# Two changes at once: expert weights loaded in 2 MB units of 16 KB per partition, and the recurrence's gate matmuls spread between the first block's projections

## What is computed

```python
def first_block(x, ...):
    h = rmsnorm(x, norm1_g)
    p = einsum('bsd,dn->bsn', h, w_in)                  # 1024 -> 1536
    lru_x, lru_gate, four_in = p[..., :512], p[..., 512:1024], p[..., 1024:]
    c = centred_depthwise_conv(lru_x, conv_w, conv_b)   # width 4
    h_f = rglru(c, ..., reverse=False)                  # gates: sigmoid of block-diagonal matmuls of c,
    h_b = rglru(c, ..., reverse=True)                   # then h[t] = a[t] h[t-1] + sqrt(1 - a[t]^2) i[t] c[t]
    y_lru = gelu(lru_gate) * (h_f + h_b)
    y_four = fourier_mix(four_in)                       # real part of a 2-D DFT
    x = x + concatenate([y_lru, y_four]) @ w_out
    h2 = rmsnorm(x, norm2_g)
    x = x + expert_choice_moe(h2, w_router, w_gate, w_up, w_down)
    return rmsnorm(x, normf_g)

def expert_choice_moe(h, ...):       # 16 experts, each takes its 64 best tokens
    gate, idx = top_k(scores, 64)
    xin = h[bidx, idx]
    g, u = xin @ w_gate[e], xin @ w_up[e]               # 1024 -> 2048 each
    eo = (silu(g) * u) @ w_down[e]                      # 2048 -> 1024
    return scatter-add of gate * eo
```

## Time and profile before

| | |
|---|---|
| median of 3 runs | 1633.52 us |
| span of the profiled execution, first to last instruction | 1631.2 us |
| 0 to 226.8 us | first block, up to the first expert's gate product |
| 226.8 to 1169.9 us | 16 experts |
| 1169.9 to 1631.2 us | second block |
| mean granted TensorE clock | 0.977 |

### The profile page before, as it was taken

One profiled execution on the slowest core, in us unless ns is written; L12 is line 12 of the kernel. 1 busy time (PEld: TensorE's weight loads), 2 busy tenths in 40 slices (PEclk: granted clock), 3 DMA queues, 4 the chain that ended last, 5 costly groups with the idle time before them and its releaser, 6 DMA issues.

```text
span 1631.2 us, 17621 instructions
## 1 busy us (share of the span) xinstructions
PE 1446.7 (89%) x6849; PEld 770.6 (47%) x6849; DVE 561.3 (34%) x998; ACT 323.8 (20%) x497; POOL 130.2 (8%) x183
## 2 busy tenths in 40 slices
PE   7988869999888888888899899889589999999997
PEld 5866623333232232233233233223278877778875
DVE  6485332011111211211201201201368477665663
ACT  4465300000000000000000000000332333233331
POOL 1030000000000000000000000000223114431001
PEclk9999979999999999999999999999899999999998
DMA  9016548999999999999999999999833211224321
GB/s 320 1 52 258 202 167 340 392 419 419 415 418 420 415 417 420 416 417 420 416 417 421 416 416 422 415 415 422 320 126 110 78 59 40 65 59 174 103 104 52
DMA packets 111258, 464.00 MB, mean 284 GB/s; under 512 B 8304, under 2 KB 35184, under 8 KB 78320
## 3 DMA queue, kind: packets, MB, share of 16 engines
q1 hardware_dynamic: 107520, 456.16, 69.9%
q0 software_dynamic: 3408, 6.82, 1.6%
q10 hardware_dynamic: 288, 0.44, 0.1%
HBM read 457.10 MB, written 6.29 MB: 284 GB/s over the span
## 4 chain that ended last, share of the span: by engine, by line
PE 56%; DMA 29%; DVE 5%; ACT 5%; issue 2%; SPq 2%; POOL 1%; POOLq 0%; DVEq 0%; ACTq 0%
DMA ring<-in_w_down 14%; DMA ring<-in_w_gate 13%; PE bank L695 12%; PE bank L541 9%; PE bank L542 9%; PE bank L543 9%; PE bank L714 5%; PE bank L673 4%; PE bank L723 3%; SPq L463 1%; DMA ring<-in_w_in 1%; PE bank L821 1%; DMA ring<-in_w_up 1%; PE bank L758 1%; PE bank L779 1%
## 5 line engine op out<-in xcount | busy, mean ns | idle before, releaser
L695 PE MATMUL bank<-ring,xinT 128*64 128x512 f32 x2016 | 441.8, 594 | 32.6 <-DVE xinT L1258 19.4
L695 PEld LDWEIGHTS bank<-ring,xinT 128*64 128x64 f32 x2016 | 144.6, 137 | 319.5 <-issue 274.9
L714 PE MATMUL bank<-ring,actT 128*64 128x512 f32 x1008 | 236.7, 607 | 41.7 <-DMA ring<-in_w_down 29.9
L1258 DVE TENSOR_TENSOR xres<-xres,bank 128x512 f32<-128x512 f32 x128 | 78.0, 681 | 306.9 <-PE bank L723 306.9
L1261 DVE SCALAR_TENSOR_TENSOR th<-th,bank 128x512 f32<-128x512 f32 x32 | 20.6, 684 | 442.9 <-ACT th L1021 442.9
L714 PEld LDWEIGHTS bank<-ring,actT 128*64 128x64 f32 x1008 | 73.9, 138 | 194.7 <-issue 92.5
L541 PE MATMUL bank<-hT_lo,ring_r 128*128 128x512 f32 x384 | 153.4, 399 | 7.6 <-DVE hT_lo L1261 7.6
L543 PE MATMUL bank<-hT_hi,ring_r 128*128 128x512 f32 x384 | 150.9, 393 | 0.0
L542 PE MATMUL bank<-hT_hi,ring_r 128*128 128x512 f32 x384 | 150.6, 392 | 0.0
L1258 DVE TENSOR_TENSOR ring_r<-ring,ring_r 128x2048 fp32r<-128x2048 f32 x37 | 85.2, 2304 | 72.9 <-ACT ring_r L909 72.9
L1021 ACT ACTIVATE th<-bank 128x512 f32<-128x512 f32 x32 | 17.4, 594 | 446.6 <-PE bank L695 446.6
(11 more groups left out here) (292 smaller groups left out, 1571.0 us busy)
## 6 DMA issues: line engine op xcount, KB each, us to landing
ring<-in_w_gate SPq DMA_DIRECT2D x126, 1024.0 KB, 20.4
ring<-in_w_up SPq DMA_DIRECT2D x126, 1024.0 KB, 20.5
ring<-in_w_down SPq DMA_DIRECT2D x126, 1024.0 KB, 20.7
ring<-in_w_in SPq DMA_DIRECT2D x26, 1024.0 KB, 5.3
ring<-in_w_out SPq DMA_DIRECT2D x8, 1024.0 KB, 4.9
xres<-in_x SPq DMA_DIRECT2D x4, 512.0 KB, 5.9
ring<-in_dft_s SPq DMA_DIRECT2D x2, 1024.0 KB, 13.7
early<-in_w_gate SPq DMA_DIRECT2D x2, 1024.0 KB, 9.5
```

The costliest lines, as they stand in the source:

```text
L695: last = pe.matmul(bank[1 + 2 * (m % 2) + q // 2][o:o + 64, :], xinT[:, k, :], w[:, q * 512:(q + 1) * 512], start=(k == 0), stop=(k == KT ...
L714: last = pe.matmul(bank[7][64 * n:64 * n + 64, :], actT[:, kt // 8 * 4 + kt % 4, at:at + 64], w[:, i, n * 512:n * 512 + 512], start=(kt == ...
L1258: return dve.tensor_tensor(out_, a, b, op)
```

## The change

Two parts. **Expert weights:** a unit is 4096 float32 per partition (2 MB). The same 12 slots' space is seen as 6 slots `wide0` to `wide5`, an expert is 12 units (8 gate and up, 4 down), 3 early areas replace 6. In a unit, partition p gets rows 2p and 2p+1 of a block of 256 (gate, up) or rows 4p to 4p+3 of a block of 512 (down), so that its 16 KB lie together in memory. So that the rows fit, the transposes of `xg` take every second column and those of `act` every fourth, and the gain `g2` is laid out the same way (`g2w`, 8 more columns). The number of products and of bytes stays. **First block:** `order_b1` puts lru0 behind in2, lru1 behind in4, the `four` products behind in7, lru2 behind them, lru3 behind in10, and all four `mix` last. The gate weights go to slot 5 and are the third weight unit loaded, the last `w_in` unit goes to slot 6, and ACT's and DVE's orders follow; the square roots become `roots_of(c)`, placed behind the next projection's copy. The GELU's tanh steps move before the last two `mix` copies.

```diff
-E_UNITS = 24
-EARLY = 6
+WIDE = 2 * UNIT
+E_UNITS = 12
+WIDE_RING = RING // 2
+EARLY = 3
...
-        order_b1 = [("in", n) for n in range(9)] + [("four", c) for c in range(CT)] + [
-            ("lru", 0), ("in", 9), ("in", 10), ("lru", 1), ("in", 11), ("lru", 2), ("mix", 0), ("mix", 1),
-            ("lru", 3), ("mix", 2), ("mix", 3)]
+        order_b1 = [("in", 0), ("in", 1), ("in", 2), ("lru", 0), ("in", 3), ("in", 4), ("lru", 1), ("in", 5), ("in", 6),
+                    ("in", 7)] + [("four", c) for c in range(CT)] + [
+            ("lru", 2), ("in", 8), ("in", 9), ("in", 10), ("lru", 3), ("in", 11)] + [("mix", g) for g in range(CT)]
+        W_LRU = 5
+        in_units = (0, 1, 2, 3, 4, 6)
...
             def load_expert(e, m, dst, arrived):
-                if m < KT * 2:
-                    w, k = (w_gate, w_up)[m % 2], m // 2
-                    src = w[bass.ds(e, 1), k * P:(k + 1) * P, :].rearrange("a p n -> p (a n)")
+                if m < KT:
+                    w, j = (w_gate, w_up)[m % 2], m // 2
+                    src = w[bass.ds(e, 1), 2 * j * P:(2 * j + 2) * P, :].rearrange("a (p i) n -> p (a i n)", i=2)
                 else:
-                    j = m - 2 * KT
-                    src = w_down[bass.ds(e, 1), 2 * j * P:(2 * j + 2) * P, :].rearrange("a (i p) n -> p (a i) n", i=2)
-                    dst = dst.rearrange("p (i n) -> p i n", i=2)
+                    j = m - KT
+                    src = w_down[bass.ds(e, 1), 4 * j * P:(4 * j + 4) * P, :].rearrange("a (p i) n -> p (a i n)", i=4)
                 sp.dma_start(dst, src).then_inc(arrived, 16)
...
-                if n < RING:
-                    former = B1_UNITS + n - RING
-                elif n < 2 * RING + EARLY:
-                    former = B1_UNITS + n - RING - EARLY
+                s = moe_slot(n)
+                if n < WIDE_RING:
+                    former = 2 * s + 1 if s else B1_UNITS - 1
+                elif n < 2 * WIDE_RING + EARLY:
+                    former = B1_UNITS + n - WIDE_RING - EARLY
                 else:
-                    former = B1_UNITS + n - RING
+                    former = B1_UNITS + n - WIDE_RING
                 sp.wait_ge(unit_used, former + 1)
...
                 for j in range(4):
-                    last = pe.transpose(bank[0][:, j * P:(j + 1) * P], xg[:, j * P:(j + 1) * P], ident)
+                    last = pe.transpose(bank[0][:, j * P:(j + 1) * P],
+                                        xg[:, 2 * P * (j // 2) + j % 2:2 * P * (j // 2 + 1):2], ident)
...
-                for m in range(2 * KT):
-                    k, w = m // 2, arrived(m)
-                    for q in range(4):
+                for m in range(KT):
+                    w = arrived(m).rearrange("p (i n) -> p i n", i=2)
+                    for i in range(2):
+                        k = 2 * (m // 2) + i
+                        for q in range(4):
...
                     for q in range(4):
-                        last = pe.transpose(bank[5 + b][:, q * P:(q + 1) * P], act[:, b, q * P:(q + 1) * P], ident)
+                        last = pe.transpose(bank[5 + b][:, q * P:(q + 1) * P], act[:, b, q:4 * P:4], ident)
...
+            project_out(0)
+            project_out(1)
+            weights_hi(2)
+            project_out(2)
+            gates(0)
+            project_out(3)
+            weights_hi(3)
+            roots_of(0)
+            project_out(4)
+            gates(1)
+            project_out(5)
+            weights_hi(4)
+            roots_of(1)
+            project_out(6)
+            project_out(7)
...
+            weights_hi(6)
+            gates(2)
+            project_out(8)
+            roots_of(2)
+            project_out(9)
             weights_hi(7)
-            act_e.wait_ge(k_ready, 1)
-            gates(0)
-            project_out(9)
+            weights_hi(8)
             project_out(10)
-            gates(1)
+            gates(3)
             project_out(11)
-            weights_hi(8)
-            gates(2)
+            roots_of(3)
             mix_out(0)
+            for c in range(CT - 1):
+                gelu_tanhs(c)
             mix_out(1)
-            gates(3)
+            gelu_tanhs(CT - 1)
+            weights_hi(9)
             mix_out(2)
-            weights_hi(9)
             mix_out(3)
...
+            convolved(0)
+            convolved(1)
+            weights_lo(2)
+            convolved(2)
+            recurrences(0)
+            weights_lo(3)
+            convolved(3)
+            recurrences(1)
+            weights_lo(4)
```

More of the change, by code:

```diff
@@ L147, in build @@
         ring_r = [area_r(f"ring{s}_r", s * UNIT, UNIT) for s in range(RING)]
+        wide = [area(f"wide{s}", s * WIDE, WIDE) for s in range(WIDE_RING)]
         xres = area("xres", RING * UNIT, TT, D)
@@ L197, in build @@
         assert ends["logT"] <= ends["eo"]
-        early = [area(f"early{i}", ends["eo"] + i * UNIT, UNIT) for i in range(EARLY - 2)]
-        early += [area(f"early{EARLY - 2 + i}", ends["nrm"] + i * UNIT, UNIT) for i in range(2)]
+        early = [area(f"early{i}", ends["eo"] + i * WIDE, WIDE) for i in range(EARLY - 1)]
+        early.append(area(f"early{EARLY - 1}", ends["nrm"], WIDE))
         qT = area("qT", 0, CT, S)
@@ L252, in build @@
         ring_full = [sem(f"ring_full{s}") for s in range(RING)]
+        wide_full = [sem(f"wide_full{s}") for s in range(WIDE_RING)]
         early_in = [sem(f"early_in{i}") for i in range(EARLY)]
@@ L432, in load @@
                     v = unit - MOE_END
-                    last = last_of[s] if v < RING2 else unit - RING2
+                    last = last_of[s // 2] if v < RING2 else unit - RING2
                     sp.wait_ge(unit_used, last + 1)
@@ L707, in expert @@
                 bank_free(7, 1)
[L708 to L712 removed]
+                for j in range(4):
+                    w = arrived(KT + j).rearrange("p (i n) -> p i n", i=4)
+                    for i in range(4):
+                        at = 64 * (j % 2)
                         for n in range(2):
[L714 to L715 removed]
+                            last = pe.matmul(bank[7][64 * n:64 * n + 64, :], actT[:, j // 2 * 4 + i, at:at + 64],
+                                             w[:, i, n * 512:n * 512 + 512], start=(j == 0 and i == 0),
+                                             stop=(j == 3 and i == 3))
                     last.then_inc(unit_used, 1)
@@ L1301, in _, with convolved @@
             dve.tensor_scalar(kneg, kpos, -1.0, None, ALU.mult).then_inc(k_ready, 1)
-            for c in range(CT):
+            def convolved(c):
                 was_read(dve, f"in{c}")
@@ L1310, in _ @@
                 last.then_inc(conv_ready, 1)
-                if c in (1, 3):
-                    weights_lo(2 if c == 1 else 3)
-            weights_lo(4)
-            weights_lo(5)
-            for c in range(CT):
-                for half in range(2):
-                    name = f"four{c}_{half}"
-                    g = slice(2 * half, 2 * half + 2)
-                    high_stands(dve, name)
-                    read(name, tt(four_lo[:, c, g, :].rearrange("p a b -> p (a b)"), bank[jobs.bank(name)][:, :],
-                                  four_hi[:, c, g, :].rearrange("p a b -> p (a b)"), ALU.subtract))
             def recurrences(c):
```

143 lines of the change are left out of this document (75 added, 68 removed).

## The result

The changed kernel takes 1594.97 us (median of 4 runs, 1594.08 to 1595.76) against 1633.22 us for the kernel before, measured beside it (4 runs, 1632.79 to 1634.46). The ratio is 0.9766, with a 95% interval of 0.9752 to 0.978: 38.3 us faster. The forecast was 1599.8 us, range 1591 to 1613. The span of the profiled execution fell from 1631.2 to 1593.9 us.

A forecast was written before the change was run, and what follows sets the result against it. DMA bounds thirteen of sixteen experts; the first block loses to TensorE gaps and clock. First block 14.4 + DMA stretch 21.0 - later start 1.7 = 33.7 us, off 1633.5: 1599.8 us, range 1591 to 1613.

The forecast's parts named there:

- The row law: Expert weight loads: 2.41 us per MB plus 9.4 ns per row of an engine, so 58.8 us per expert, not 60.24.
- The rival that nothing above 8 KB is faster: Expert loads: 16 KB rows move no faster than 8 KB ones, 59.7 us per expert, 1612.7 us in all; chance 0.13.
- free row starts: Expert loads, bound of the estimate: if a row's start cost nothing at all, 57.9 us per expert.
- 21.0 us over the stretch: Experts, where DMA never stops: 174 units at 4.90 us take 852.6 us instead of 873.6, 21.0 less.
- Begins 1.7 us later: Start of the unbroken DMA stretch in expert 1: the first slot comes free only when 2 MB are used, 1.7 us later.
- The last unit's end is hidden: End of the experts: the last 2 MB take TensorE 3.5 us instead of 1.9, hidden behind the second block's loads.
- The ring: Between experts: six slots do not starve DMA, margin at least 2.4 us; rival of coarse ring or costly transposes, chance 0.10.
- five units that need no new slot: Between experts: these queued units keep DMA busy for 24.5 us, against a need of at most 22.1.
- Strided transposes: Experts' 12 transposes with strided columns: taken as costing nothing, upper bound 5.4 us per expert; slower rival 1648 us, chance 0.03.
- The first block: TensorE's gaps and clock losses: 15.26 us can go, less 0.8 for a new wait, gain 14.4 us.
- Unit 3's low part: First block's tight place on VectorE: ready at 55.3 us, in6 starts at 58.0, margin 2.7; new-wait rival 1607 us, chance 0.13.
- The new wait of the `four` products: First block: these products follow in7 at once and wait for its copy, costing 0.8 us.

The follow-up runs named there:

- e3: Changed kernel with 2 MB expert units made of the old short rows (8 KB gate and up, 4 KB down), transposes without stride: 1619.82 us, ratio 0.9922.
- e4: Changed kernel with a ring of 4 slots of 2 MB instead of 6: 1627.1 us in one run.
- e2: Changed kernel with the expert units put back to 1 MB, so only the first block's new order remains: 1619.66 us, ratio 0.992.
- e6: Changed kernel with the transposes of `act` reading every eighth float instead of every fourth: 1598.76 us in one run.
- e5: Kernel before with 8 or 16 unused zero columns of constants added, moving areas by 32 or 64 bytes: 1633.59 and 1634.84 us, one run each.
- e8: The changed kernel run once more, word for word: 1596.55 us, ratio 0.9779 to the kernel before.

## Why the prediction was right, point by point

- **The row law.** 4.90 us for a 2 MB unit and 58.8 us for an expert were forecast; 58.74 came, 4.894 per unit. The law, read off rows of 1, 4 and 8 KB, held at 16 KB, and e3 gave the old pace back by the row length alone. The 40960 packets that e3 has more are 2560 on each of 16 DMA engines, 160 for each expert; at the law's 9.4 ns that is 1.50 us, and 60.24 - 58.74 is 1.50. The rival that nothing above 8 KB is faster (59.7) falls, free row starts (57.9) too. The Trainium skill's best load of 425 GB/s ("DMA: Bandwidth & Descriptors", section "Measured (HBM→SBUF, 128 partitions, SWDGE, issued from GpSimd)") was passed here at 428.
- **21.0 us over the stretch.** It was 22.7, the largest error of size in the experts. Of it, 348 x 2.510 - 174 x 4.894 = 873.5 - 851.6 = 21.9 are the units themselves, since 4.90 was 0.006 us too much 174 times (and the prediction's 873.6 is 0.1 too much for its own product). The other 0.8 is what lies around them, 4.8 us before and 4.0 after; no run here takes that apart.
- **Begins 1.7 us later.** It did by 1.86: 271.43 - 210.79 = 60.64 us behind expert 0's first product, before 285.58 - 226.80 = 58.78. Of this 1.71 are the larger slot (3.69 - 1.98), and in the other 0.15 expert 1's first product comes later (56.95 us behind expert 0's instead of 56.80), about what the strided transposes cost an expert.
- **The last unit's end is hidden.** 28.38 and 28.39 us: right.
- **The ring.** No starvation, as forecast, but the margin of 2.4 us was too small a figure, and not for a wrong need: e4 puts that at about 21 us, within the 22.1 forecast. The step that was off is the cover, "five units that need no new slot": it leaves out the last unit's own slot, free and refilled 3.7 us behind its landing. With it there are six units, 29.4 us, and some 8 us of margin. The forecast of e4 took over the same miscount. It did no harm to the time, since it erred on the safe side.
- **Strided transposes.** Taken as nothing; they cost 0.18 us of TensorE's time per expert (55.09 to 55.27), hidden from expert 3 on. In time the value was right, in mechanism not: every strided load does pay. The rule weighed there ("SBUF — State Buffer", "Door 1: The DMA port swizzle") would have a step of two floats free and one of four dear; the rows show 208 and 210 ns, so the trace does not agree with it for loads of weights.
- **The first block.** 14.4 was forecast and 14.2 came from the order alone (e2). Unit 3's low part, the tight place, was done at 54.4 us in the changed kernel. VectorE's timeline:

```profile
52.12 2.29 DVE L1290 TENSOR_TENSOR ring_r<-ring,ring_r 128x2048 fp32r<-128x2048 f32 x1
```

  55.3 was forecast, from rows of an execution that was 1.5 us later at this point of the block; in e6, which is later by the same, it was done at 55.9. The copy of in5, by which the prediction dates in6, starts at 57.46 us in the changed kernel, so the margin was 3.0 us (forecast 2.7), and TensorE did not wait. The new wait of the `four` products was 0.9 us, forecast 0.8.
- **What was not in the sum.** The span fell by 3.6 us more than the 33.7. In the first block 1.6: 1.5 of start clock, which is an execution's luck and not the change's work, and 0.44 of operand places, less 0.2 from the order and 0.1 elsewhere. In the experts 1.5, as above. In the second block 0.45, from operand places (e5). The median fell further by 1.2, as it stands 1.1 us above the span here and stood 2.3 above it before; e8, the same program, has 1.9. Of the rivals, the faster pace rules out the rows that gain nothing; no wait came in the first block but the one in the sum; the strided loads cost something, but hidden; and the ring never starved.

## What to carry to other kernels

When a stage is bound by DMA at a steady pace, fit bytes and rows from the loads that the trace already has: a law from three row lengths gave the fourth to 0.1%, and it says that the layout of the memory side (which rows a partition takes) is the lever, not the size or number of transfers (e3). A contraction lets the rows go to any partition, so the price is only a stride in the transposes, 70 ns for a load. Test a coarser ring by making it coarser still: a kernel with two slots fewer showed the margin, and its issue rows showed which unit the arithmetic had left out. And at the level of 1 to 2 us, compare places between equal granted clocks before giving a difference to an edit.

## What the runs showed of the hardware that was not expected

- Where the operands of a product lie can count: shifting the areas by 32 bytes took the 48 products of an output unit from 11.25 to 11.09 us, and a shift of 64 bytes did not (11.20). A stretch of the second block went from 67.1 to 66.15 us with it, and the last one from 56.3 to 56.9.
- A strided read of a TensorE weight load of 128 columns costs 208 to 210 ns at steps of 2 and 4 floats and 194 at 8, against 140 without a step.
- Two executions of one program differ in TensorE's granted clock at given places: 1.00 or 0.83 and 0.74 at the start (1.5 us), 1.00 or 0.83 for 10 us of the second block (1.6 us), 1.00 or 0.83 for 10 us of expert 0 between programs whose work there is the same (1.7 us).
- A row of 16 KB went as one packet: 40960 packets fewer for the same bytes (63488 against 104448), 1.50 us per 24 MB.
- In a ring, the unit in use frees its own slot in time to be refilled: a ring of four covers four units behind the last landing, 19.6 us, where 21.1 were needed.
